# Fixed PSUM banks for logits, flips and values in two attentions, and one attention part behind each weight unit

## The reference

```
q, k, v, g, f = split(h @ w_in)               # 1024 -> 4 * 1024 + 16
q = rms_norm(q, q_gain) * 64 ** -0.5 ; k = rms_norm(k, k_gain)
cum = cumsum(log_sigmoid(f + b_f))
for qs in (0, 128):
    logits = q[qs:qs+128] @ k[:qs+128].T + cum[queries] - cum[keys]
    p = softmax(where(causal, logits, -inf))
    outs.append(p @ v[:qs+128])
y = (o * silu(g)) @ w_out
```

## Time and profile before

| | |
|---|---|
| Median of 3 runs | 747.31 us |
| Profiled execution, its own time | 747.15 us |
| Span of the profiled execution | 745.3 us |
| Mean granted clock of TensorE | 0.988 of full speed |
| TensorE matmul busy | 713.5 us, 96% |
| VectorE busy | 503.2 us, 68% |
| ScalarE busy | 379.8 us, 51% |

### The profile page before, as it was taken

One profiled execution on the slowest core, in us unless ns is written; L12 is line 12 of the kernel. 1 busy time (PEld: TensorE's weight loads), 2 busy tenths in 40 slices (PEclk: granted clock), 3 DMA queues, 4 the chain that ended last, 5 costly groups with the idle time before them and its releaser, 6 DMA issues.

```text
span 745.3 us, 9411 instructions
## 1 busy us (share of the span) xinstructions
PE 713.5 (96%) x3556; PEld 584.8 (78%) x3556; DVE 503.2 (68%) x723; ACT 379.8 (51%) x559; POOL 22.8 (3%) x37
## 2 busy tenths in 40 slices
PE   6999999999999899988899899999999999999996
PEld 6887787777877677766688788888887888888884
DVE  3889878788836678554467779966675455555444
ACT  5447445556445565534445754554566444444343
POOL 6000000000000000000001200000000000000000
PEclk9999999999999999999899999999999999999998
DMA  9999775666963557632245453343465556655521
GB/s 297 371 361 314 257 248 171 200 210 236 315 206 113 196 172 249 231 113 69 74 142 169 145 170 109 115 140 116 139 199 183 184 172 196 192 182 185 193 67 56
DMA packets 74476, 138.96 MB, mean 186 GB/s; under 512 B 5748, under 2 KB 18272, under 8 KB 74432
## 3 DMA queue, kind: packets, MB, share of 16 engines
q1 hardware_dynamic: 72816, 134.82, 55.5%
q10 hardware_dynamic: 736, 1.90, 0.7%
q0 software_dynamic: 880, 1.64, 0.7%
HBM read 137.31 MB, written 1.05 MB: 186 GB/s over the span
## 4 chain that ended last, share of the span: by engine, by line
PE 84%; DVE 8%; ACT 3%; issue 3%; DMA 1%; SPq 0%; DVEq 0%; ACTq 0%
PE G L360 22%; PE G L362 22%; PE G L361 22%; PE T L381 4%; PE T L860 2%; PE T L747 2%; DVE wlo L1035 2%; PE T L737 1%; DVE arena L1035 1%; DMA arena<-in_mod_w_dram 1%; ACT whi L1776 1%; DVE arena L1044 1%; ACT arena L1778 1%; PE G L471 1%; DVE st L1408 1%
## 5 line engine op out<-in xcount | busy, mean ns | idle before, releaser
L1035 DVE TENSOR_TENSOR wlo<-raw,whi 128x1024 fp32r<-128x1024 f32 x206 | 251.0, 1222 | 133.2 <-ACT whi L1776 132.4
L360 PE MATMUL G<-whi,ahi 128*128 128x512 f32 x776 | 316.7, 408 | 4.7 <-DVE wlo L1035 4.2
L362 PE MATMUL G<-whi,alo 128*128 128x512 f32 x776 | 305.5, 394 | 0.0
L361 PE MATMUL G<-wlo,ahi 128*128 128x512 f32 x776 | 304.7, 393 | 0.0
L1776 ACT ACTIVATE whi<-raw 128x1024 fp32r<-128x1024 f32 x206 | 217.2, 1059 | 130.8 <-PE G L362 118.2
L360 PEld LDWEIGHTS G<-whi,ahi 128*128 128x128 f32 x776 | 147.4, 190 | 37.4 <-DVE wlo L1035 7.1
L362 PEld LDWEIGHTS G<-whi,alo 128*128 128x128 f32 x776 | 147.1, 190 | 32.6
L361 PEld LDWEIGHTS G<-wlo,ahi 128*128 128x128 f32 x776 | 147.6, 190 | 29.3 <-issue 1.4
L1778 ACT ACTIVATE arena<-T,st 128x128 f32<-128x128 f32 (+2 forms) x56 | 22.4, 473 | 51.5 <-DVE st L1408 51.5
L381 PE MATMUL T<-head,arena 128*128 128x128 f32 x244 | 37.0, 277 | 2.0 <-ACT arena L1778 2.0
L381 PEld LDWEIGHTS T<-head,arena 128*128 128x128 f32 x244 | 29.6, 142 | 10.4 <-ACT arena L1778 2.1
(11 more groups left out here) (219 smaller groups left out, 579.8 us busy)
## 6 DMA issues: line engine op xcount, KB each, us to landing
raw<-in_ret_w_in_dram SPq DMA_DIRECT2D x48, 512.0 KB, 5.3
raw<-in_w_gate_up_dram SPq DMA_DIRECT2D x40, 512.0 KB, 3.9
raw<-in_mod_w_dram SPq DMA_DIRECT2D x32, 512.0 KB, 5.0
raw<-in_fox_w_in_dram SPq DMA_DIRECT2D x32, 512.0 KB, 4.8
raw<-in_w_in_dram SPq DMA_DIRECT2D x28, 512.0 KB, 3.6
raw<-in_w_down_dram SPq DMA_DIRECT2D x22, 512.0 KB, 4.4
arena<-in_mod_w_dram SPq DMA_DIRECT2D x16, 512.0 KB, 8.8
raw<-in_ret_w_out_dram SPq DMA_DIRECT2D x16, 512.0 KB, 5.4
```

Source lines behind the costliest of these rows:

```text
L360: e.matmul(o, ah, wh, start=first and k == 0, stop=False)
L361: e.matmul(o, ah, wl, start=False, stop=False)
L362: done = e.matmul(o, al, wh, start=False, stop=last and k == 1)
L1035: e.tensor_tensor(o, a, b, op).then_inc(sig[name], 1)
```

## The change

`attention_steps` returns a list of parts (n + 2 of them) in place of a flat list; part i holds logits i, flip i - 1 and values i - 2. In FOX one part stands behind each unit: part 0 behind the fourth unit ahead of the old start (behind `gate_rows`), part 1 + k behind the old first unit and those after it, and part 13 behind the last unit along with part 12. WIN keeps its slices, on the flattened list.

`bank` takes a bank number in place of `hold`; with one given, the counter `at` stays. In both attentions logits of an even group take bank 0, of an odd group bank 1, flips bank 2, values bank 3. The first two left operands of FOX and the first of WIN take bank 2. `gated_fox(0)` now stands ahead of part 10 on VectorE; it stood behind that part's first step. Values 8, flip 10 and values 9 come a unit earlier than they did; logits 10 and 11, flips 9 and 11 and values 10 stay behind their unit.

```
 def attention_steps(n):
-    out = []
-    for i in range(n + 2):
-        out += [("logits", i)] * (i < n) + [("flip", i - 1)] * (1 <= i <= n) + [("values", i - 2)] * (i >= 2)
-    return out
+    return [[("logits", i)] * (i < n) + [("flip", i - 1)] * (1 <= i <= n) + [("values", i - 2)] * (i >= 2) for i in range(n + 2)]
...
-            def bank(name, sem, n, hold=False):
-                while at[0] % 4 in held:
+            def bank(name, sem, n, i=None):
+                if i is None:
+                    i = at[0] % 4
                     at[0] += 1
-                i = at[0] % 4
-                at[0] += 1
                 if ring[i] is not None:
                     on_.wait_ge(*ring[i])
...
-                t = [bank((name, "logits", g + z), sig[f"{name}_exp"], g + z + 1) for z in range(2)]
+                t = [bank((name, "logits", g + z), sig[f"{name}_exp"], g + z + 1, z) for z in range(2)]
...
-                t = bank((name, "values", g), sig[f"{name}_out"], 2 * g + 2)
+                t = bank((name, "values", g), sig[f"{name}_out"], 2 * g + 2, 3)
...
-                t = bank((name, "flip", g), sig[f"{name}_turned"], g + 1)
+                t = bank((name, "flip", g), sig[f"{name}_turned"], g + 1, 2)
...
+            def attend(part):
+                for what, g in steps[part]:
+                    fox[what](g)
...
                 elif k == 3:
                     gate_rows(1, GATE1, gate[:, 1, :])
+                    attend(0)
...
-                for what, g in steps[3 * k:3 * k + 3]:
-                    fox[what](g)
+                attend(1 + k)
...
-                for what, g in steps[12 + 3 * k:15 + 3 * k]:
-                    fox[what](g)
+                attend(5 + k)
...
-                for what, g in steps[(24, 27, 29, 31)[k]:(27, 29, 31, 34)[k]]:
-                    fox[what](g)
-                if k == 2:
-                    left_of(0, 0)
-            left_of(2, 0)
-            for what, g in steps[34:]:
-                fox[what](g)
+                attend(9 + k)
+                if k >= 2:
+                    left_of(2 * k - 4, 0, 2)
+            attend(13)
...
-                    left_mix(0, ("win_out", 8))
+                    left_mix(0, ("win_out", 8), 2)
```

VectorE and ScalarE get the same parts at the same units:

```
                 if k == 1:
-                    fox[part[0][0]](part[0][1])
                     gated_fox(0)
-                    part = part[1:]
-                for what, g in part:
-                    fox[what](g)
-                if k == 2:
-                    left_low(8)
-            left_low(10)
-            for what, g in steps[34:]:
-                fox[what](g)
+                attend(9 + k)
+                if k >= 2:
+                    left_low(2 * k + 4)
+            attend(13)
...
                 elif k == 3:
                     gate_copies(1)
+                    weights_of("fox", FOX, PBf, steps[0])
```

More of the change, by code:

```diff
@@ L328, in _ @@
             ring = [None] * 4
-            held = set()
             at = [0]
@@ L344, in bank @@
                 bank_of[name] = i
-                if hold:
-                    held.add(i)
                 return T[i]
@@ L548, in _, with left @@
             lefts = [0]
-            def left(tiles, slot, sem, n):
+            def left(tiles, slot, sem, n, at_bank=None):
                 on_.wait_ge(sig[sem], n)
                 i = lefts[0] = lefts[0] + 1
-                t = bank(("left", i), sig["left_lo"], i)
+                t = bank(("left", i), sig["left_lo"], i, at_bank)
                 transposes(t, tiles, "left_turned")
@@ L774, in _, with left_of @@
             fox = {"logits": fox_logits, "flip": lambda g: flip("fox", g, PBf), "values": fox_values}
-            def left_of(k, c):
+            def left_of(k, c, at_bank=None):
                 left([of[:, m, 2 * (k + i):2 * (k + i) + 2, :].rearrange("p h n -> p (h n)") for i in range(2) for m in range(2)],
-                     8 + k, "fox_gated", 2 * c + 2)
+                     8 + k, "fox_gated", 2 * c + 2, at_bank)
+            def attend(part):
+                for what, g in steps[part]:
+                    fox[what](g)
             accs = pair(0)
@@ L920, in _, with left_mix @@
                 freed(0, m, "vaw", m + 1)
-            steps = attention_steps(len(WIN))
+            steps = sum(attention_steps(len(WIN)), [])
             win = {"logits": win_logits, "flip": lambda g: flip("win", g, PBw), "values": win_values}
[L925 to L928, removed]
+            def left_mix(k, done, at_bank=None):
+                left([mix[:, m, (k + i) * P:(k + i + 1) * P] for i in range(2) for m in range(2)], k, *done, at_bank)
             accs = pair(1)
@@ L1456, in _ @@
                 u += 1
-                for what, g in steps[12 + 3 * k:15 + 3 * k]:
-                    fox[what](g)
+                if k == 3:
+                    attend(0)
+            for k in range(8):
+                ring_to(u + 2)
+                u += 1
+                attend(1 + k)
             for k in range(4):
@@ L1461, in _ @@
                 u += 1
-                part = steps[(24, 27, 29, 31)[k]:(27, 29, 31, 34)[k]]
                 if k == 1:
-                    fox[part[0][0]](part[0][1])
                     gated_fox(0)
-                    part = part[1:]
-                for what, g in part:
-                    fox[what](g)
-                if k == 2:
-                    left_low(8)
-            left_low(10)
-            for what, g in steps[34:]:
-                fox[what](g)
+                attend(9 + k)
+                if k >= 2:
+                    left_low(2 * k + 4)
+            attend(13)
             for n in range(4):
@@ L2067, in _ @@
                 u += 1
-                weights_of("fox", FOX, PBf, steps[3 * k:3 * k + 3])
+                weights_of("fox", FOX, PBf, steps[1 + k])
             fox_va(1, 1)
@@ L2072, in _ @@
                 u += 1
-                weights_of("fox", FOX, PBf, steps[12 + 3 * k:15 + 3 * k])
+                weights_of("fox", FOX, PBf, steps[5 + k])
             fox_silu(0, 0)
@@ L2077, in _ @@
                 u += 1
[L2078 to L2081, removed]
+                weights_of("fox", FOX, PBf, steps[9 + k])
+                if k >= 2:
+                    left_high(2 * k + 4)
             fox_silu(1, 1)
-            weights_of("fox", FOX, PBf, steps[34:])
             for n in range(4):
```

## The result

The kernel after takes 736.34 us (median of 4 runs, 734.31 to 738.9) against 746.45 us of the kernel before on the same chip: a ratio of 0.9866, 95% interval 0.9829 to 0.9902. The forecast was 738.2 us, in a range of 734 to 742.5. Five later runs of the same kernel gave 0.9861 (0.9836 to 0.9886). The profiled execution took 735.73 us, with a span of 733.9 us (before 745.3).

The account below looks back on a forecast made before the run. TensorE, busy 96% of the span, was taken as the bound, with waits and a slow clock in the forgetting attention. 13.90 us removed, 4.0 of new waits and 0.8 for the clock gave -9.1 us: 738.2 us, range 734 to 742.5.

Parts of the forecast that it names:

- Step 1: Forgetting attention: values in their own bank 3 lose 7.20 us of waits ahead of values 1, 3, 5, 7.
- Step 2: Forgetting attention: logits 0 and 1 issued a unit sooner, so the 1.95 us wait ahead of flip 0 goes.
- Step 3: Forgetting attention: with the waits gone, the slow clock's 4.75 us are given back; bounds 0 and 4.75.
- Step 4: Forgetting attention: logits 2 and 3 need bank 1, so exp 1; new wait of 0.95 us, bounds 0 and 1.5.
- Step 5: Forgetting attention: earlier gating delays flip 10's copy, so the first left operand waits 1.0 us for bank 2; bounds 0, 1.6.
- Step 6: Forgetting attention: values 10 and 11 share a bank; left transposes between hide the normalisation: 0 us, bounds 0 and 0.6.
- Steps 7 and 8: Window attention: new waits of 1.0 us ahead of flip 1 and 1.05 us ahead of values 5.
- Step 9: Both attentions: each new wait could lower the clock once, at 1.59 us; half a fall taken, 0.8 us, bounds 0, 6.4.
- Rival A: Forgetting attention: values don't wait for their bank; only 1.95 us go and 4.0 come: 749.2 us, chance 0.03.
- rival B: Both attentions: single flip and value banks pass VectorE's lateness to TensorE at all 36 uses: 755.2 us, chance 0.06.
- rival C: Both attentions: the clock doesn't come back, or falls after the new waits: 742.1 to 743.8 us, chance 0.16.
- rival D: Forgetting attention: the new waits don't come there, and no fall: 735.5 us, down to 733.5, chance 0.10.

Follow-up runs that it names:

- best version: Kernel after with its four new waits removed, gating of the first half one unit split earlier and values 11 in bank 0: 731.65 us, ratio 0.9805.

## Why the prediction was right, step by step

- Step 1, the values' bank: right. No odd values wait, with the banks alone too, and the wait put back takes the gain away. The guess that exp 3 ends just ahead of values 1 holds, by 0.14 us. Logits 10 didn't wait for exp 9: the cover of 0.5 us held (0.45 in the trace after).
- Step 2, flip 0: right, the 1.95 us are gone. But by itself it was worth nothing: with the ring the next bank took back 1.47 of it, and values 9 another 0.81.
- Step 3, the clock: right, 4.75 us forecast and given back. Filling the waits alone gives the same 4.75, within a shortening of 5.02 us.
- Step 4, logits 2 behind exp 1: forecast 0.95, measured 0.84 us.
- Step 5, the left operand behind the copy of flip 10: forecast 1.0, measured 1.31 us, within its bounds; both ways of cutting the chain remove it.
- Step 6, values 11: right while the left operand waits ahead of it; 0.43 us show when it doesn't.
- Steps 7 and 8, the window attention: forecast 1.0 and 1.05, measured 0.94 and 0.97 us (for the first, 500.08 - 499.13 is 0.95, which I had taken as 1.0). The Trainium skill's advice of another bank while one is read (PSUM — Partial Sum Buffer, Summary: rules for kernel authors) agrees with the trace in just these places, and in the places with a unit between two uses the trace shows no cost.
- Step 9, the clock behind the new waits: 0.8 us taken, none came in this profile. That was luck of the one execution: a fall followed the 1.06 us ahead of values 5 with the banks alone and the 0.97 us with the wait put back, and none followed it in the later trace of the kernel after. So a part of a fall was the right size to take for this step.

By the medians the change is -10.1 us, against -9.1 forecast; the spans of the two profiled executions differ by -11.4. The 2.3 us between -9.1 and -11.4 are: 0.8 of step 9; 1.58 for the fall in the residual stage, which this execution of the kernel before had and this one of the kernel after had not; and 0.68 more saved in the forgetting attention. Against them stand about 0.46 for the slower starts behind the two waits of the window attention, 0.23 us for the later start and 0.06 for the sizes of the new waits. The first two terms are chance: the later trace has the residual fall, and its span gives -10.3. For the 0.68 I have this much: an odd part with a wait takes 0.23 us more than its wait and its work (1.48 against 1.25), 0.9 us over four, less some 0.1 to 0.2 us for each of the two new waits there. The filled waits don't bring most of it back (0.05 to 0.08 us a part), so this extra is worked out and not explained. My sum put it at nothing.

Rival A fell with the run with the banks alone, rival B with the missing waits at 34 of the 36 uses (its price also took the new waits twice, since the 9.9 us already have them off), rival C with the granted clock of 1.00 in the forgetting attention, and rival D with the waits of steps 4 and 5, which came. The median of 736.34 lies nearer to D's 735.5 than to the forecast, but not by D's mechanism; 0.9 of the 1.9 us from the forecast is that a fourth run moved the median of before from 747.31 to 746.45.

## What to carry to other kernels

When banks go round a ring, ask of each user which result its bank last held and how late that is read: here parts took four and two banks in turn, so every second values step landed on the logits read last, and a fixed bank per kind of result removed that wait without another bank. It costs where two results of a kind stand next to each other, so fix banks only in the stage that waits, and let what reads last be read first. An earlier start of a chain gives nothing while the next wait is set by another engine.

## What the runs showed of the hardware that I had not expected

The same wait doesn't bring the clock down each time. The clearest case is the 1.24 us wait in the residual stage, which all twelve traces have at the same place: the clock fell behind it in seven of them (before among them, and one of the two of the unchanged kernel after) and not in the other five. Ahead of values it fell behind 1.77, 1.41 and 3.22 us before, behind 1.78 us in the run with the schedule alone and not behind the 2.27 us there (busy table below, the unit after it), not behind 1.33 us with the wait put back, but behind 1.06 us in the run with the banks alone and once behind the 0.97 us ahead of the window's values 5, which four other traces have without a fall. So in these traces the price of a wait was its length, 0.1 to 0.23 us for the start behind it, and in some executions about 1.6 us for a fall. What decides whether a fall comes stays open.

```profile
330.40:334.50 4.10, 4.10 (x31) 3.15 (x31) 1.74 (x3) 0.00 (x0) 0.00 (x0) 1.00 0.33 98
```

Runs differ most ahead of the attention, where no two versions differ: the gate rows start between 307.61 us (best version) and 312.24 us (window attention on the ring). The span of the one is 726.5 us and of the other 735.4, 8.9 us apart, of which this start is 4.6. The two ran on different chips, but on one chip it also varies, by 2.1 us between the best version and the kernel after beside it. What sets it stays open; a stretch of the trace tells versions apart that the times can't.
